# Order of work around the first seven-product column pair: snapshots and weight halves before the silu steps, two low parts moved on GpSimd, the fourth weight's low part before the first's

## What is computed

```python
def conv_ffn(h, w_up, conv_w, conv_b, w_down):
    L = h.shape[1]
    up = h @ w_up                                   # 1024 -> 2 x 2816
    up_p = jnp.pad(up, ((0, 0), (CONV_WIDTH - 1, 0), (0, 0)))
    c = conv_b + sum(conv_w[j] * up_p[:, j:j + L] for j in range(CONV_WIDTH))
    gate, val = jnp.split(c, 2, axis=-1)
    return (jax.nn.silu(gate) * val) @ w_down
```

## Time and profile before

| | us |
|---|---|
| median of 3 runs | 1266.1 (1265.87 to 1266.59) |
| the profiled execution, its own time | 1271.5 |
| its span | 1269.7 |
| TensorE busy | 1210.7 (95%) |
| VectorE busy | 801.9 (63%) |
| ScalarE busy | 687.6 (54%) |
| GpSimd busy | 616.7 (49%) |

### The profile page before, as it was taken

One profiled execution on the slowest core, in us unless ns is written; L12 is line 12 of the kernel. 1 busy time (PEld: TensorE's weight loads), 2 busy tenths in 40 slices (PEclk: granted clock), 3 DMA queues, 4 the chain that ended last, 5 costly groups with the idle time before them and its releaser, 6 DMA issues. The chain is left out here.

```text
span 1269.7 us, 25047 instructions
## 1 busy us (share of the span) xinstructions
PE 1210.7 (95%) x9927; PEld 1148.7 (90%) x9927; DVE 801.9 (63%) x1263; ACT 687.6 (54%) x1255; POOL 616.7 (49%) x365
## 2 busy tenths in 40 slices
PE   5899999988999988999999999999997999999998
PEld 5889999988999988999989898889986999997886
DVE  8898222899999986111455555554699999986002
ACT  7997443445666664222556665633255666664223
POOL 5433566453444435565655455319663444435431
PEclk9899999997999999999999999999997999999999
DMA  8333333233333323333221211112332344313231
GB/s 174 64 75 70 113 95 91 68 83 89 112 100 101 100 63 91 88 89 112 69 77 54 64 51 51 51 35 84 100 84 67 103 114 115 104 67 101 99 110 73
DMA packets 179541, 109.47 MB, mean 86 GB/s; under 512 B 7100, under 2 KB 173789, under 8 KB 179165
## 3 DMA queue, kind: packets, MB, share of 16 engines
q1 hardware_dynamic: 179141, 107.83, 30.7%
q10 hardware_dynamic: 288, 0.07, 0.0%
HBM read 101.59 MB, written 2.10 MB: 82 GB/s over the span
## 5 line engine op out<-in xcount | busy, mean ns | idle before, releaser
L386 POOL TENSOR_TENSOR wL<-raw,wH 128x1024 fp32r<-128x1024 f32 (+1 forms) x114 | 278.3, 2444 | 346.1 <-ACT wH L382 320.3
L1073 PE MATMUL ps<-FB,wH 128*128 128x264 f32 (+1 forms) x1904 | 354.7, 287 | 20.7 <-ACT snap L1741 11.3
L1073 PEld LDWEIGHTS ps<-FB,wH 128*128 128x128 f32 x1904 | 303.2, 194 | 22.5 <-ACT snap L1741 11.7
L1073 PE MATMUL ps<-FB,wL 128*128 128x264 f32 (+1 forms) x952 | 274.4, 288 | 0.0
L382 ACT ACTIVATE wH<-raw 128x1024 fp32r<-128x1024 f32 (+1 forms) x114 | 119.1, 1046 | 234.6 <-PE ps L1164 87.1
L1073 PEld LDWEIGHTS ps<-FB,wL 128*128 128x128 f32 x952 | 183.2, 192 | 0.0
L2780 POOL TENSOR_TENSOR wL<-raw,wH 128x1024 fp32r<-128x1024 f32 x34 | 82.7, 2432 | 117.7 <-ACT wH L1697 117.7
L2780 POOL TENSOR_TENSOR wL<-Wsum,wH 128x1024 fp32r<-128x1024 f32 x34 | 82.4, 2424 | 77.9 <-ACT wH L1697 77.9
L2419 DVE SCALAR_TENSOR_TENSOR ps<-u,PV,ps 128x528 f32<-128x528 f32 (+1 forms) x136 | 103.1, 758 | 2.9 <-ACT ps L1779 1.8
L1278 PE MATMUL ps<-hgH,wH 128*128 128x264 f32 x384 | 83.2, 298 | 0.0
L1278 PE MATMUL ps<-hgH,wL 128*128 128x264 f32 x384 | 78.2, 285 | 0.0
(11 more groups left out here) (353 smaller groups left out, 3050.4 us busy)
## 6 DMA issues: line engine op xcount, KB each, us to landing
raw<-ffn_w_up SPq DMA_DIRECT2D x88, 512.0 KB, 4.5
raw<-ffn_w_down SPq DMA_DIRECT2D x38, 512.0 KB, 3.4
raw<-attn_w_qkv SPq DMA_DIRECT2D x24, 512.0 KB, 3.7
raw<-s_w_glu SPq DMA_DIRECT2D x16, 512.0 KB, 4.1
TT<-KD SPq DMA_DIRECT2D x64, 64.0 KB, 2.4
raw<-attn_w_o SPq DMA_DIRECT2D x8, 512.0 KB, 3.9
raw<-ffn_w_down SPq DMA_DIRECT2D x8, 384.0 KB, 3.4
xb<-x SPq DMA_DIRECT2D x8, 256.0 KB
```

The costliest lines, as they stand in the source:

```text
L386: nc.gpsimd.tensor_tensor(wL[:, slot, 0:nk], raw[:, slot % 2, 0:nk], wH[:, slot, 0:nk].bitcast(F32), ALU.subtract).then_inc(w_lo, 1)
L1073: mm = nc.tensor.matmul(ps[:, bank, 0:width], w[:, at, k, :], x[:, k], start=first and k == 0 and i == 0, stop=k == 3 and i == 2, skip_gro ...
```

## The change

It reorders four lists and adds or removes no instruction.

- ScalarE: S1's rounded part of pair 0 is made before the taps of plain pair 3, and A22's and the first snapshot of pair 0 before the silu of plain pair 2. The silu of pair 3 moves from pair 0's round into pair 1's, behind its first snapshot. The third snapshot of pair 0 comes before the taps of pair 4.
- VectorE: `factor_low(F_T3)` before `drain(3)`; `factor_low(F_T1)` before the taps of pair 2; S1's low part of pair 0 before the last taps of pair 2, where it came after all taps of pair 3; `multiply(3)` from pair 0's round to pair 1's; and in every round the low part of S4 before that of S1, with the table to match.
- GpSimd: the low part of `F_B22` before that of the last plain unit, that of `F_T4` right after it, and then AA and S23 of pair 0.

```diff
@@ low_places
     for s in range(FAST):
-        order += [("S1", s)] + ([("S4", s - 1)] if s else []) + [("A22", s)]
+        order += ([("S4", s - 1)] if s else []) + [("S1", s), ("A22", s)]
@@ ScalarE, ffn
                 sums_23(0)
+                sum_1(0)
                 plain_taps(3)
+                direct_last(0)
+                first_snap(0)
                 plain_silu(2)
                 for s in range(FAST):
                     more = s + 1 < FAST
-                    sum_1(s)
+                    if s:
+                        sum_1(s)
                     if s >= 2:
                         silu(s - 2)
-                    direct_last(s)
+                    if s:
+                        direct_last(s)
                     if s >= 2:
                         val_in(s - 2)
-                    first_snap(s)
-                    if s == 0:
+                    if s:
+                        first_snap(s)
+                    if s == 1:
                         plain_silu(3)
@@
                     else:
+                        third_snap(0)
                         plain_taps(4)
-                    if s == 0:
-                        third_snap(0)
@@ VectorE, ffn
                 multiply(1)
+                factor_low(F_T3)
                 drain(3)
-                factor_low(F_T3)
+                factor_low(F_T1)
                 n = plain_taps(2, 1)
-                factor_low(F_T1)
+                weight_low("S1", 0)
                 after(n)
                 n = plain_taps(2, 0)
                 sum_4(0)
@@
                 multiply(2)
-                weight_low("S1", 0)
                 drain(4)
                 for s in range(FAST):
                     more = s + 1 < FAST
                     if s:
                         bottom_right(s - 1)
                     if s:
+                        weight_low("S4", s - 1)
                         weight_low("S1", s)
-                        weight_low("S4", s - 1)
                     weight_low("A22", s)
@@
                     elif s == 1:
+                        multiply(3)
                         n = plain_taps(4, 1)
@@
-                    if s == 0:
-                        multiply(3)
-                    elif s == 1:
+                    if s == 1:
                         after(last)
                         multiply(4)
@@ GpSimd, ffn
-                for j in range(4, 2 * PLAIN):
+                for j in range(4, 2 * PLAIN - 1):
                     split_lo(pool, nu + j, (nu + j) % 4)
+                factor_low(F_B22, 11)
+                split_lo(pool, nu + 2 * PLAIN - 1, (nu + 2 * PLAIN - 1) % 4)
+                factor_low(F_T4, 12)
                 weight_low("AA", 0)
-                factor_low(F_B22, 11)
                 weight_low("S23", 0)
-                factor_low(F_T4, 12)
```

More of the change, by code:

```diff
@@ L2506, in ffn @@
                         sum_2(s + 1)
-                    if s == 0:
-                        multiply(3)
-                    elif s == 1:
+                    if s == 1:
                         after(last)
                         multiply(4)
-                    else:
+                    elif s:
                         bank_multiply(s - 2, last)
```

## The result

| | before | changed |
|---|---|---|
| median | 1265.66 us (10 runs, 1264.9 to 1268.31) | 1269.38 us (10 runs, 1269.05 to 1269.62) |
| ratio | | 1.0028, 95% interval 1.0018 to 1.0037 |
| profiled execution, its span | 1271.5, 1269.7 | 1269.51, 1267.7 |

The account below looks back on a forecast made before the run. VectorE's arrival at `bottom_left(0)` was taken to bound the hand-over. Layer 0: -0.7 + 2.25 = +1.55; layer 1: -0.2 + 2.25 = +2.05; together +3.6 on 1266.1 gives 1269.7 us, 8-in-10 range 1263.5 to 1273.0.

Parts of the forecast that it names:

- The row that decides: P1 of pair 2 on TensorE waits for VectorE's `bottom_left(0)`; idle and slow time ahead of it is worth nothing.
- Part 1: GpSimd's order before `bottom_left(0)`: its eight subtractions hold VectorE 14.4 us in sum, +0.4 against before.
- what the prediction left open: Whether `sum_1`, two SBUF inputs and PSUM output, is held; if free, the sum of holds 0.6 lower at most.
- 16.8 less 14.0: Upper end for VectorE's holds, all eight subtractions held for their full length: given as +2.7.
- part 2: VectorE's order before `bottom_left(0)`: its waits of 0.67 and 0.53 us go, -1.1 in layer 0.
- Part 3: TensorE's old stalls before P6 and P3 go; a new wait of about 3.6 us before P1 of pair 2.
- The 0.9 us that I gave S23: TensorE's remaining wait for S23 of pair 1, ahead of P1 of pair 2: some 0.9 us.
- Part 4: Half clock on TensorE behind the new wait before P1 of pair 2: 2.25 us lost in each layer.
- The sum: Both layers: -0.7 + 2.25 = +1.55 and -0.2 + 2.25 = +2.05, together +3.6 us.
- the first: Rival: behind the new wait the clock holds or falls in one layer alone; 1265.2 to 1267.5 us, chance 0.22.
- gained two covers: Rival: GpSimd's subtractions meet one or two more PSUM instructions, VectorE gains 1.2 each; 1262.4 us, chance 0.15.
- lost one: Rival: S23 of pair 0 misses `drain(3)` or the last unit comes sooner, 1.1 more holds per layer; 1273.0, chance 0.13.

Follow-up runs that it names:

- version 2: The kernel before with 36 extra matmuls before P6 and 20 before P3 of pair 0, filling the old waits: 1266.72 us, ratio 1.0003.
- version 8: Kernel before with GpSimd's new order, ScalarE's early snapshots, `bottom_left(0)` right behind plain pair 4's taps, S4 before S1, 12 extra matmuls: 1263.89 us, ratio 0.9985.
- version 9: version 8 without its 12 extra matmuls before P3 of pair 1, all else the same: 1264.16 us, ratio 0.9987.
- version 10: The changed kernel with the edits of version 8: 1264.55 us, ratio 0.9993.
- Version 1: The changed kernel with 28 extra matmuls in each layer, filling the new wait before P1 of pair 2: 1265.68 us, ratio 0.9996.
- version 4: The changed kernel with S4's low part put back behind S1's in every round: 1266.80 us, ratio 1.0005.
- Version 6: The kernel before with only ScalarE's early first snapshot of pair 0, ahead of the silu of pair 2: 1266.21 us, ratio 1.0000.
- versions 5 and 7: The kernel before with GpSimd's new order alone (5: 1265.82 us, ratio 0.9999), and with ScalarE's early first snapshot too (7: 1265.94 us, ratio 1.0005).

## Why the prediction was right

- **The row that decides.** Right. P1 of pair 2 starts 0.1 us behind `bottom_left(0)` after; filling the waits ahead of it does not show in the time (version 2; 0.6 us in the profile of layer 0), and the versions with `bottom_left(0)` 4 us further forward (8 and 9) are the only ones whose time is clearly under before's (version 10, with the same move, has an interval that reaches 1.0003).
- **Part 1, the holds.** 14.4 us forecast. The rows above give 4.58 - 1.44 = 3.14 (two holds), 3.51 - 1.25 = 2.26, 2.77 - 0.69 = 2.08, 2.21 - 1.25 = 0.96, 2.12 in the four taps at 285.23, 2.13 - 0.69 = 1.44 and 2.90 - 0.69 = 2.21: 14.2. Single places differ: B22 did not hold `multiply(0)` but a tap behind `drain(2)`, and T4 fell on the factor of 3.51. AA of pair 2 fell on `sum_1(2)`, and that settles what the prediction left open: an instruction with two SBUF inputs is held when its output goes to PSUM too (2.90 against 0.69). The Trainium skill (SBUF — State Buffer, "Who interferes with whom") states the rule by the inputs alone, two in SBUF against a GpSimd instruction that reads SBUF; this row agrees. Two small slips of the prediction: 16.8 less 14.0 is 2.8, not 2.7, which moves one end alone, and the waits of part 2 were 1.2 and entered as 1.1.
- **Part 2, the waits.** Right: the view shows no idle time of VectorE from 262.86 to 308.93. `bottom_left(0)` came 0.95 us sooner in layer 0 (0.7 forecast) and, against its own segment, 0.4 in layer 1 (0.2 forecast).
- **Part 3, the stalls.** P1 of pair 0 at 279.30 (279.2 forecast), P1 of pair 1 at 292.18 (292.2) after 4.47 us (4.7), no wait for S4. P1 of pair 0 in layer 1 waited for `drain(3)` 2.1 us longer than before, as forecast (4.28 against 2.18). The 0.9 us that I gave S23 was there in layer 1 alone, as 0.58, so TensorE was ready for P1 of pair 2 at 305.20 (305.6 forecast), and the new wait is 3.84 and 4.09 us (3.6).
- **Part 4, the clock.** 2.7 and 1.5 us lost, 4.2 together, where the forecast took 4.5 as two middle values. Neither layer lost the 2.25 that it was given; the two errors nearly cancel. Version 1 shows that the clock is the whole of the slowdown. The Trainium skill (TensorE: Matmul & The Clock Gate, "Terms") has the throttled time x (1 - K/N): an estimate of 3.0 and 1.7 here, from the busy time at half clock. The rows stand 0.2 to 0.3 under it.
- **The sum.** Layer 0: -0.95 + 2.7 = +1.75, measured +1.68. Layer 1: -0.4 + 1.5 = +1.1, measured +1.13. Together +2.8 in the segments. The medians give +3.7 (2.3 to 4.7 by the interval), nearer to the forecast's +3.6; the difference of 0.9 is within that interval and was not traced. So the mechanism and the signs came out as laid down, the size was 0.8 too large in the segments, and that the medians meet it within 0.1 us is luck.
- **The rivals.** The clock fell in both layers, so the first did not come true; version 4 shows how close it was, 2.77 us of idle time with the clock at full. VectorE neither gained two covers nor lost one.
- **What the prediction did not see.** It took the change's edits together. It did not say that the loss hangs on S4's move: with S4 left where it was, the rest is at no change.

What stays open: why GpSimd's order makes the segments 1.55 us shorter and the median hardly. Each version has one profile, and the profiles point at one source of spread: half clock behind short waits outside the hand-over. Version 6's profile (1267.98, the median 1266.21) has it behind a wait of 1.36 us at 1130.2 us, and its last stretch is 1.4 us longer than in the others. Whether that makes the spread of versions 5 and 7 is not shown.

## What to carry to other kernels

When one engine sets the time of a stretch, look for its instruction that the other one next waits for, and ask of every edit whether that instruction comes sooner; here stalls of 5 to 6 us could go without any gain. TensorE's short stalls ahead of such a point also do something: they shorten the wait at it. Taking them away gathers the idle time in one piece behind which the clock falls, and there nothing covers it. What helped here is to reorder the setting engine's queue so that the awaited instruction comes first (version 8, 2.4 us under before with 4 us of move, of which the segments put about half down to GpSimd's order), or to keep TensorE at work through the wait (version 1, 3.7 us under the changed kernel, and no gain over before).

## What the runs showed of the hardware that was not expected

- **The length of a wait does not decide by itself whether the clock falls behind it.** 2.76 us of idle time before were followed by half clock, and 2.70 in layer 1 of the changed kernel too (its half clock from 960.12 to 963.53); in version 4, 2.77 and 2.70 were not. In version 9, 1.90 us were, and 1.92 were not; in layer 1, 2.18 us before the first product were not in before, and were in version 2. At the two hand-overs every wait of 2.97 us or more was. Below, it goes further down than these places show: behind a wait of 1.36 to 1.39 us that every profile has near 1130 us, it fell in one of twelve (version 6). A forecast for waits of 1.4 to 2.8 us should carry both outcomes.
- **Which of two waiting engines goes first.** In the changed kernel B22 on GpSimd started at 260.96, while VectorE was in a factor's low part (to 261.08). The next on VectorE, `multiply(0)` at 261.01, still passed with its clean 0.69 us, and GpSimd took 3.07 for 1056 columns, where its shortest rows in this stretch took 2.4 for 1024. With T4 it went the other way: T4 started at 266.83, during a tap of VectorE, took 2.92, and the factor behind the tap was held (3.51). No run tells what decides between the two.
- **A subtraction of GpSimd costs VectorE 2.0 to 2.3 us where only instructions with two SBUF inputs meet it, and 1.0 to 1.7 where reads of PSUM lie in its time** (the 1.7 in version 5): 14.2 us in 48 here. Over all orders that were run the sum of the eight stayed between 13.4 and 14.3 us in each layer.
